# The first output projection in three split passes, its differential half begun inside the attention

## The chip, the cores and the metric

The kernel runs on one core of a Trainium2 chip, in one launch. The metric is the device time of that core in microseconds (us), the median of the runs. Five engines run their own instruction streams and meet at semaphores: TensorE (PE: matmuls and transposes, operands from SBUF, results into one of eight PSUM banks), VectorE (DVE), ScalarE (ACT), GpSimd (POOL) and SyncE (SP: it issues DMAs from memory in the order of its program, and a wait in it holds all loads behind it).

## The reference, cut to what matters

Two layers of a transformer over 256 latent tokens and 256 context tokens, model width 1024, all in float32. The even layer computes

- `qa, ka, va, qb, kb, vb = split(t @ w_in)`, with a root-mean-square norm per head of 64 on the queries and keys;
- eight neighbourhood attention heads with a position bias and a mask, and four differential heads: `pd = softmax(q0 k0) - lam * softmax(q1 k1)`, `out_b = rms_norm(pd @ vb, subln_g) * (1 - lam_init)`;
- `y = concat(out_a, out_b) @ w_out`, with `w_out` 1024 x 1024, for latent and context tokens alike (512 columns together);
- `x = x + gate * y`, a norm over the width, a modulation per token group, and a dense SwiGLU of width 2816.

The odd layer has two other attentions, its own output projection and a choice of two of eight experts. The change is about the line `y = concat(out_a, out_b) @ w_out` of the even layer.

## The kernel before, in words

Everything is held transposed: activations are `[128 partitions, 8 tiles k, 512 tokens]`, a weight tile 128 x 128 is the stationary operand and 512 tokens are the moving one. A product in full float32 is one matmul call, which TensorE runs as two passes. A product in split form takes each operand as a high part, which is the value rounded into the type fp32r, and a low part, which is the remainder; three matmuls (high times high, low times high, high times low) go into the same bank. The first input projection (L1825 to L1827), the feed-forward part (`split3`, L1979 to L1981) and the experts are in split form; the attentions and both output projections (`out_pe`, L1945) are in full float32. ACT makes a high part with a copy (L1094, L1125), DVE the low part with a subtraction (L1503, L1530).

Weights pass through a ring of four slots of 2 MB. `order` lists the loads and `slot_of` the slot of each; SP waits for the work named in `released` that frees a slot. Behind the six chunks of the input projection come ("O0", 0) and ("O0", 1), the halves of `w_out` by output columns, then ("F0", 0), the first gate and up chunk of the feed-forward part in slot 2, ("A0b", 6), a chunk of modulation weights in slot 3, ("F0", 1), and so on.

The attention A0 is a list of 36 jobs, written out by `att_plan`: jobs 0 to 15 are differential pairs, the rest pairs of neighbourhood heads, and in between jobs 22, 25, 28 and 31 are "sub" jobs, one for each of the four token tiles, which norm that tile's differential output and turn it. Tiles 0 and 1 attend to 512 keys, 2 and 3 to 256. The loop of each engine goes through steps i: PE computes the scores of job i (L1890), turns the probabilities (or the sub's data) of job i-3 into banks 4 and 5 (L1907), and multiplies job i-4 with the values (L1925, L1929) into bank 6 or 7. ACT copies what was turned in job i-3 (L1038; for a sub into `hT` k = 4 to 7, L1031), takes the exponentials of job i (L1048), and copies a finished tile of head outputs into `hT` k = 0 to 3 (L1063). DVE takes the maxima of job i (L1406), mixes the pair of job i-2 (L1414), takes the reciprocals of job i-1 (L1421) or norms the sub of job i-1 (L1430, L1431), and POOL scales the probabilities of the head jobs (L885).

Then `out_pe` waits for all outputs and makes eight output tiles d, each over the eight k, in banks 0 to 3, with w_out in full float32. `out_dve` adds each tile, times its gate, to the stream (L1453) and sums squares (L1460 to L1463). While that runs ACT makes the high parts of the first two feed-forward units (`unit_high`, 128 x 1024 each), and DVE, ahead of `out_dve`, their low parts (`unit_low`, L1530) and twelve accumulation steps of modulation weights (`modulate(0)` to `modulate(2)`, L1267, L1270). The norm follows (PE L1781, ACT L950, DVE L1559), then the modulated tokens in high and low parts (L1564, ACT L1134, L1571), for which the first feed-forward matmuls wait.

```
jb = job_at(pl, i - LAG_TURN)
if jb is not None:
    pe.wait_ge(s["copied"], jb["banks0"])
...
att_pe("A0")
out_pe("O0", "A0", S_ALL, 4)
norm_pe("n01", S_ALL, sq[0])
```

Of the kernel before, what the change touches and what calls it, by code (L numbers as in the profile page):

```python
# [37 lines left out]
P = 128  # L38
# [33 lines left out]
UF = 2  # L72
# [74 lines left out]
def build_kernel(nc, a, out):  # L147
    with ExitStack() as ctx:
# [64 lines left out]
        assert 16384 == (KT + 2 * HALF_T[0]) * S_ALL  # L213
        whi = sb("whi", [P, URING, UNIT], F32R)
# [103 lines left out]
        L0_SLOTS = [0, 1, 2, 2, 0, 2, 1, 2, 0, 2, 1, 2]  # L318
# [3 lines left out]
        for j in range(6):  # L322
            order += [("F0", j), dsum[j]]
# [69 lines left out]
        for nm in ("O0", "O1"):  # L393
            outp[nm] = {k: sem(f"out{nm}_{k}") for k in ("done", "added")}
        f_hi = sem("ffn_unit_high_ready")
# [125 lines left out]
        def piece_lo(c, i):  # L521
            return ring012r[:, slot_of(at["W0", c]), i * FU:(i + 1) * FU]

# [116 lines left out]
        def att_plan(layer):  # L640
# [39 lines left out]
            pairs = groups = banks = mixes = scales = 0  # L680
            for jb in jobs:
                jb["pair"], jb["group"], jb["banks0"] = pairs, groups, banks
# [36 lines left out]
        def _(sp):  # L719
# [15 lines left out]
            for g, (nm, j) in enumerate(order):  # L735
# [12 lines left out]
                elif nm == "F0":  # L748
                    load(g, slot3(g, 256)[:, 0:KT, :], cols(a["ffn_w_gate"], 256 * j, 256))
# [188 lines left out]
        def _(act):  # L938
# [80 lines left out]
            def att_act(nm, between=lambda i: None):  # L1019
                s, pl = att[nm], plans[nm]  # L1020
                for i in range(NSTEP[nm]):
# [5 lines left out]
                    if jb is not None:  # L1027
                        for e in range(2 if jb["kind"] == "head" else 1):
                            act.wait_ge(s["turned"], jb["banks0"] + e + 1)
                            if jb["kind"] == "sub":  # L1030
                                act.activation(hT[:, 4:8, jb["t"] * P:(jb["t"] + 1) * P],  # L1031
# [21 lines left out]
                    if jb is not None and jb["last"]:  # L1053
# [8 lines left out]
                        else:  # L1062
                            act.activation(hT[:, 4 * jb["half"]:4 * jb["half"] + 4, t * P:(t + 1) * P],  # L1063
# [52 lines left out]
            att_act("A0")  # L1116
# [116 lines left out]
        def _(dve):  # L1233
# [156 lines left out]

            def att_dve(nm):
                s, pl = att[nm], plans[nm]
                for i in range(NSTEP[nm] + 1):
# [40 lines left out]
                    if jb is not None and jb["last"] and jb["kind"] == "diff":  # L1434
# [3 lines left out]
                        dve.tensor_reduce(ssf[:, 4 * t:4 * t + 4], v3(osq, P), AX.X, ALU.add).then_inc(s["ored"], 1)  # L1438
                    if nm == "A0" and i == ROOT_STEP:
# [5 lines left out]
            def out_dve(nm, l, nc_, after):  # L1445
# [3 lines left out]
                for d in range(KT):  # L1449
# [9 lines left out]
                    if d == 0:  # L1459
                        ch.after(dve.tensor_tensor(sq[0][:, 0:nt], x, x, ALU.mult))  # L1460
                        continue
                    ch.after(dve.tensor_tensor(sq[1][:, 0:nt], x, x, ALU.mult))
                    ins = dve.tensor_tensor(sq[0][:, 0:nt], sq[0][:, 0:nt], sq[1][:, 0:nt], ALU.add)  # L1463
                    if d == KT - 1:
                        ins.then_inc(norm[after]["square"], 1)
                    else:
                        ch.after(ins)
# [85 lines left out]
            for u in range(UF):  # L1553
                unit_low(u)
# [681 lines left out]
```

## Time and profile before

| | |
|---|---|
| median of 3 runs | 1923.04 us (1920.83 to 1923.13) |
| the profiled execution's own time | 1919.05 us |
| its span, first to last instruction | 1917.2 us |
| mean granted TensorE clock | 0.984 of full |
| busy: PE, DVE, ACT, POOL | 1827.5, 1358.9, 1106.5, 176.0 us |
| attention A0, PE's first score to the first output matmul | 215.28 to 304.95 us |
| output projection O0 on PE | 304.95 to about 360.2 us |
| first feed-forward matmul | 371.4 us |
| experts, from about 941 us on | one item takes about 118.5 us, PE busy throughout |

The profile is one execution; times are counted from its first instruction. A busy time of PE sums matmuls whose ends are modelled, so intervals between starts tell its pace better than durations. Idle time stands in square brackets with what ended it.

### The profile page before, as it was taken

The numbers are of one execution on the slowest core, as the hardware profiler recorded it, in microseconds if no ns is written. First come the engines' busy times: TensorE is split into PE (matmuls) and PEld (weight loads), VectorE is DVE, ScalarE is ACT, GpSimd is POOL, SyncE is SP. The second block draws the span as 40 slices with busy tenths as digits, with TensorE's granted clock in tenths as the row PEclk, the third lists the DMA queues.
The fourth block names the chain that finished last, engine by engine and source line by source line (L and its number), as shares of the span: only waits on it lengthen the run. The fifth ranks groups of instructions, "written<-read, shape, count | busy, mean of one in ns | idle before, by whom it ended". The sixth has DMA issues, their size and how long they took to land.

```text
span 1917.2 us, 24691 instructions
## 1 busy us (share of the span) xinstructions
PE 1827.5 (95%) x8660; PEld 1434.4 (75%) x8660; DVE 1358.9 (71%) x1733; ACT 1106.5 (58%) x1488; POOL 176.0 (9%) x253
## 2 busy tenths in 40 slices
PE   5999889799999999899899999999999999999999
PEld 2777564388888887557788888888888888888877
DVE  2534575567645555352699899998989989899897
ACT  3423483132222222365488888888888877887784
POOL 0114331011100100432100000000000000000010
PEclk8999999899999999999899999999999999999999
DMA  9344500478464552130399999999999999999995
GB/s 357 107 176 165 176 1 9 145 279 291 143 202 138 186 187 85 44 133 1 134 370 373 375 390 373 384 375 384 384 377 385 373 372 384 382 387 375 384 366 204
DMA packets 231538, 496.38 MB, mean 259 GB/s; under 512 B 6065, under 2 KB 43953, under 8 KB 231473
## 3 DMA queue, kind: packets, MB, share of 16 engines
q1 hardware_dynamic: 227936, 488.53, 69.6%
q0 software_dynamic: 1920, 5.77, 0.9%
q10 hardware_dynamic: 1616, 1.22, 0.2%
q8 instruction: 40, 0.66, 0.1%
q14 instruction: 26, 0.21, 0.0%
HBM read 475.05 MB, written 20.45 MB: 258 GB/s over the span
## 4 chain that ended last, share of the span: by engine, by line
PE 84%; DVE 5%; ACT 3%; DMA 3%; issue 2%; POOL 1%; SPq 1%; DVEq 0%; ACTq 0%; POOLq 0%
PE ps L2142 9%; PE ps L2144 9%; PE ps L2143 9%; PE ps L1979 6%; PE ps L1981 6%; PE ps L1980 6%; PE ps L2156 5%; PE ps L2154 5%; PE ps L2155 5%; PE ps L1945 4%; PE ps L1871 2%; PE ps L1825 2%; DMA ring<-in_moe_w 2%; PE ps L1827 2%; PE ps L1826 2%
## 5 line engine op out<-in xcount | busy, mean ns | idle before, releaser
L1617 DVE TENSOR_TENSOR wlo<-ring,whi 128x1024 fp32r<-128x1024 f32 x672 | 795.9, 1226 | 87.6 <-ACT whi L1170 78.3
L1170 ACT ACTIVATE whi<-ring 128x1024 fp32r<-128x1024 f32 x672 | 691.6, 1057 | 182.8 <-DMA ring<-in_moe_w 81.0
L2142 PE MATMUL ps<-whi,xgr 128*128 128x512 f32 x896 | 354.1, 395 | 1.5 <-DVE xgr L1695 1.5
L2144 PE MATMUL ps<-whi,xgr 128*128 128x512 f32 x896 | 350.0, 391 | 0.0
L2143 PE MATMUL ps<-wlo,xgr 128*128 128x512 f32 x896 | 349.4, 390 | 0.0
L2144 PEld LDWEIGHTS ps<-whi,xgr 128*128 128x128 f32 x896 | 168.6, 188 | 36.0
L2142 PEld LDWEIGHTS ps<-whi,xgr 128*128 128x128 f32 x896 | 168.6, 188 | 35.1 <-issue 1.7
L2143 PEld LDWEIGHTS ps<-wlo,xgr 128*128 128x128 f32 x896 | 168.8, 188 | 33.7
L1125 ACT ACTIVATE fsa<-ring 128x1024 fp32r<-128x1024 f32 (+2 forms) x76 | 71.8, 946 | 192.6 <-PE ps L1981 192.6
L2154 PE MATMUL ps<-whi,hidr 128*128 128x512 f32 x448 | 175.9, 393 | 0.0
L2156 PE MATMUL ps<-whi,hidr 128*128 128x512 f32 x448 | 174.5, 390 | 0.0
L2155 PE MATMUL ps<-wlo,hidr 128*128 128x512 f32 x448 | 174.4, 389 | 0.0
L1979 PE MATMUL ps<-hTh,fsa 128*128 128x512 f32 x352 | 139.9, 398 | 8.5 <-DVE hTl L1571 8.5
L1981 PE MATMUL ps<-hTl,fsa 128*128 128x512 f32 x352 | 137.8, 392 | 0.0
L1270 DVE SCALAR_TENSOR_TENSOR scr<-ring,scond,scr 128x512 f32<-128x512 f32 x140 | 99.4, 746 | 1.1
L1530 DVE TENSOR_TENSOR fsa<-ring,fsa 128x1024 fp32r<-128x1024 f32 (+2 forms) x38 | 42.9, 1128 | 80.4 <-ACT fsa L1125 80.3
L1530 DVE TENSOR_TENSOR fsb<-ring,fsa 128x1024 fp32r<-128x1024 f32 (+2 forms) x38 | 41.2, 1085 | 81.8 <-ACT fsa L1125 81.8
L2156 PEld LDWEIGHTS ps<-whi,hidr 128*128 128x128 f32 x448 | 84.1, 188 | 17.6
L2155 PEld LDWEIGHTS ps<-wlo,hidr 128*128 128x128 f32 x448 | 84.2, 188 | 17.0
L2154 PEld LDWEIGHTS ps<-whi,hidr 128*128 128x128 f32 x448 | 84.1, 188 | 16.8
L1979 PEld LDWEIGHTS ps<-hTh,fsa 128*128 128x128 f32 x352 | 66.5, 189 | 26.7 <-issue 8.3
L1945 PE MATMUL ps<-hT,ring 128*128 128x512 f32 (+1 forms) x256 | 84.6, 488 | 1.4 <-ACT hT L1063 1.4
(271 smaller groups left out, 2560.1 us busy)
## 6 DMA issues: line engine op xcount, KB each, us to landing
ring<-in_moe_w SPq DMA_DIRECT2D x168, 2048.0 KB, 9.8
ring<-in_ada_w SPq DMA_DIRECT2D x24, 2048.0 KB, 12.7
ring<-in_ev_w_in SPq DMA_DIRECT2D x6, 2048.0 KB, 8.0
ring<-in_ffn_w_gate SPq DMA_DIRECT2D x11, 1024.0 KB, 5.4
ring<-in_ffn_w_up SPq DMA_DIRECT2D x11, 1024.0 KB, 8.0
expert_tokens<-work SPq DMA_DIRECT2D x2, 3072.0 KB, 17.7
ring<-in_ffn_w_down SPq DMA_DIRECT2D x4, 1536.0 KB, 8.7
ring<-in_ffn_w_down SPq DMA_DIRECT2D x4, 1280.0 KB, 8.4
```

What stands on the lines that cost most here:

```text
L1170: act.activation(whi[:, u % URING, :], mslot[(u // 4) % MRING][:, (u % 4) * UNIT:(u % 4 + 1) * UNIT], ACT.Copy).then_inc(m_hi, 1)
L1617: dve.tensor_tensor(wlo[:, u % URING, :], mslot[(u // 4) % MRING][:, (u % 4) * UNIT:(u % 4 + 1) * UNIT], whi[:, u % URING, :].bitcast(F32) ...
L1945: ins = pe.matmul(ps[d % nb][:, 0:nt], w[:, k, (d % 4) * P:(d % 4 + 1) * P], hT[:, k, 0:nt], start=(k == 0), stop=(k == KT - 1))
L1979: pe.matmul(bank, wh, xh, start=first, stop=False)
L1980: pe.matmul(bank, wl, xh, start=False, stop=False)
L1981: return pe.matmul(bank, wh, xl, start=False, stop=last)
L2142: pe.matmul(bank[:, :], xgr[:, 0, kk, :], hi[:, ws], start=(kk == 0), stop=False)
L2143: pe.matmul(bank[:, :], xgr[:, 0, kk, :], lo[:, ws], start=False, stop=False)
L2144: ins = pe.matmul(bank[:, :], xgr[:, 1, kk, :], hi[:, ws], start=False, stop=(kk == KT - 1))
L2154: pe.matmul(ps[z][:, :], hidr[:, 0, f, :], hi[:, ws], start=(f == 0), stop=False)
L2155: pe.matmul(ps[z][:, :], hidr[:, 0, f, :], lo[:, ws], start=False, stop=False)
L2156: ins = pe.matmul(ps[z][:, :], hidr[:, 1, f, :], hi[:, ws], start=False, stop=(f == FTE - 1))
```

## The change

O0 is computed in split form. Its weight half 0 is split during the attention: ACT writes the high parts (128 x 1024, four pieces) in its steps 4, 6, 8 and 10 into ring slot 2, and DVE overwrites the weights in slot 0 with the low parts in its steps 26, 28, 30 and 32. Half 1 is split after the attention, the high parts into the place of the attention's values (`o0wh`). The attention's outputs go into `hTh` (fp32r), and DVE makes their low parts `outl` out of PSUM: for each sub (`sub_lo`) and each tile of head outputs (`out_lo`). PE may not turn into bank 4 again before `sub_lo`, and not begin the group of values after next before `out_lo`.

In PE's steps 36 to 39 the differential half (k = 4 to 7) of output tiles 0 to 3 is computed, one tile a step, ahead of that step's turn and values. After the attention come the head halves (k = 0 to 3) of tiles 0 to 3, then tiles 4 to 7 whole.

Since slot 2 holds the high parts, ("F0", 0) is loaded only after four output tiles, and SP's order is now ("A0b", 6), ("F0", 0), ("F0", 1), ... The first two feed-forward units' low parts move behind output tile 5, `modulate(0)` and `modulate(1)` behind tiles 3 and 4, and `modulate(2)` behind the modulated tokens.

Added and removed lines, with 8 spaces of indentation taken off:

```diff
@@ -211,6 +211,10 @@
+with ExitStack() as scope:
+    scope.enter_context(nc.sbuf_tensor("below_values", [P, SLOT + 8192], F32))
+    o0wh = scope.enter_context(nc.sbuf_tensor("o0wh", [P, SLOT], F32R))
@@ -315,11 +319,12 @@
-L0_SLOTS = [0, 1, 2, 2, 0, 2, 1, 2, 0, 2, 1, 2]
+L0_SLOTS = [0, 1, 2, 2, 0, 2, 1, 2, 0, 2, 1, 2] + [0, 1, 3, 2]
-for j in range(6):
+order += [dsum[0], ("F0", 0)]
+for j in range(1, 6):
@@ -392,6 +397,10 @@
+o_hi = sem("output_weights_high_ready")
+o_lo = sem("output_weights_low_ready")
+sub_lo = sem("differential_outputs_low_ready")
+out_lo = sem("head_outputs_low_ready")
@@ -520,6 +529,19 @@
+def o_piece(h, i):
+    return piece(at["O0", h], i)
+def o_piece_hi(h, i):
+    return (o0wh if h else ring012r[:, slot_of(at["F0", 0]), :])[:, i * FU:(i + 1) * FU]
+def o_piece_lo(h, i):
+    return ring012r[:, slot_of(at["O0", h]), i * FU:(i + 1) * FU]
+outl = hidh[:, 0:KT, :]
@@ -677,8 +699,11 @@
-    pairs = groups = banks = mixes = scales = 0
+    pairs = groups = banks = mixes = scales = subs = 0
+        jb["subs"] = subs
+        subs += jb["kind"] == "sub"
@@ -746,6 +771,9 @@
+            if j == 0:
+                sp.wait_ge(outp["O0"]["done"], 4)
@@ -1028,7 +1056,7 @@
-                        act.activation(hT[:, 4:8, jb["t"] * P:(jb["t"] + 1) * P],
+                        act.activation(hTh[:, 4:8, jb["t"] * P:(jb["t"] + 1) * P],
@@ -1060,7 +1088,7 @@
-                    act.activation(hT[:, 4 * jb["half"]:4 * jb["half"] + 4, t * P:(t + 1) * P],
+                    act.activation((hTh if nm == "A0" else hT)[:, 4 * jb["half"]:4 * jb["half"] + 4, t * P:(t + 1) * P],
@@ -1113,7 +1141,20 @@
-    att_act("A0")
+    def output_hi(h, i):
+        if i == 0:
+            g = at["O0", h]
+            act.wait_ge(slot_full[slot_of(g)], 16 * loads_upto(g))
+        act.activation(o_piece_hi(h, i), o_piece(h, i), ACT.Copy).then_inc(o_hi, 1)
+    def between(i):
+        if i in (4, 6, 8, 10):
+            output_hi(0, (i - 4) // 2)
+    att_act("A0", between)
+    for i in range(4):
+        output_hi(1, i)
@@ -1387,6 +1428,11 @@
+    def output_low(h, i):
+        dve.wait_ge(o_hi, 4 * h + i + 1)
+        dve.tensor_tensor(o_piece_lo(h, i), o_piece(h, i), o_piece_hi(h, i).bitcast(F32), ALU.subtract)\
+           .then_inc(o_lo, 1)
@@ -1436,13 +1482,28 @@
+            if nm == "A0" and i in (26, 28, 30, 32):
+                output_low(0, (i - 26) // 2)
+            jb = job_at(pl, i - LAG_TURN)
+            if jb is not None and jb["kind"] == "sub":
+                ts = slice(jb["t"] * P, (jb["t"] + 1) * P)
+                dve.wait_ge(s["copied"], jb["banks"])
+                dve.tensor_tensor(outl[:, 4:8, ts], v3(ps[4][:, :], P), hTh[:, 4:8, ts].bitcast(F32), ALU.subtract)\
+                   .then_inc(sub_lo, 1)
+            jb = job_at(pl, i - LAG_PV - 1)
+            if nm == "A0" and jb is not None and jb["last"] and jb["kind"] == "head":
+                ts = slice(jb["t"] * P, (jb["t"] + 1) * P)
+                dve.wait_ge(s["out"], jb["t"] + 1)
+                dve.tensor_tensor(outl[:, 0:4, ts], v3(ps[6 + jb["group"] % 2][:, :], P),
+                                  hTh[:, 0:4, ts].bitcast(F32), ALU.subtract).then_inc(out_lo, 1)
-    def out_dve(nm, l, nc_, after):
+    def out_dve(nm, l, nc_, after, between=lambda d: None):
@@ -1456,15 +1517,14 @@
-            if d == 0:
-                ch.after(dve.tensor_tensor(sq[0][:, 0:nt], x, x, ALU.mult))
-                continue
-            ch.after(dve.tensor_tensor(sq[1][:, 0:nt], x, x, ALU.mult))
-            ins = dve.tensor_tensor(sq[0][:, 0:nt], sq[0][:, 0:nt], sq[1][:, 0:nt], ALU.add)
-            if d == KT - 1:
-                ins.then_inc(norm[after]["square"], 1)
-            else:
-                ch.after(ins)
+            ch.after(dve.tensor_tensor(sq[min(d, 1)][:, 0:nt], x, x, ALU.mult))
+            if d:
+                ins = dve.tensor_tensor(sq[0][:, 0:nt], sq[0][:, 0:nt], sq[1][:, 0:nt], ALU.add)
+                if d == KT - 1:
+                    ins.then_inc(norm[after]["square"], 1)
+                else:
+                    ch.after(ins)
+            between(d)
@@ -1550,11 +1610,17 @@
-    for u in range(UF):
-        unit_low(u)
-    for v in range(UF + 1):
-        modulate(v)
-    out_dve("O0", 0, 2, "n01")
+    for i in range(4):
+        output_low(1, i)
+    def between(d):
+        if d in (3, 4):
+            modulate(d - 3)
+        if d == 5:
+            for u in range(UF):
+                unit_low(u)
+    out_dve("O0", 0, 2, "n01", between)
@@ -1571,8 +1637,7 @@
+    modulate(2)
@@ -1893,6 +1958,8 @@
+                if nm == "A0" and jb["subs"]:
+                    pe.wait_ge(sub_lo, jb["subs"])
@@ -1917,6 +1984,8 @@
+                        if nm == "A0":
+                            pe.wait_ge(out_lo, g - 1 - pl["squares"])
@@ -1929,6 +1998,17 @@
+    def out0_tile(d, ks):
+        h = d // 4
+        for k in ks:
+            ws = slice(k % 2 * 512 + d % 4 * P, k % 2 * 512 + (d % 4 + 1) * P)
+            wh, wl = o_piece_hi(h, k // 2)[:, ws], o_piece_lo(h, k // 2)[:, ws]
+            pe.matmul(ps[d % 4][:, :], wh, hTh[:, k, :], start=(k == 4), stop=False)
+            pe.matmul(ps[d % 4][:, :], wl, hTh[:, k, :], start=False, stop=False)
+            ins = pe.matmul(ps[d % 4][:, :], wh, outl[:, k, :], start=False, stop=(k == 3))
+        return ins
@@ -1969,8 +2049,30 @@
-    att_pe("A0")
-    out_pe("O0", "A0", S_ALL, 4)
+    NJ = len(plans["A0"]["jobs"])
+    def between(i):
+        d = i - NJ
+        if not 0 <= d < 4:
+            return
+        if d == 0:
+            pe.wait_ge(o_lo, 4)
+            pe.wait_ge(sub_lo, 4)
+        if d in (0, 2):
+            pe.wait_ge(att["A0"]["exp"], 2 * len(plans["A0"]["pairs"]) - 2 + d)
+        out0_tile(d, range(4, KT))
+    att_pe("A0", between=between)
+    pe.wait_ge(att["A0"]["out"], plans["A0"]["outs"])
+    pe.wait_ge(out_lo, 4)
+    for d in range(KT):
+        if d == 4:
+            pe.wait_ge(o_lo, 8)
+        if d >= 4:
+            pe.wait_ge(outp["O0"]["added"], d - 3)
+            out0_tile(d, range(4, KT))
+        out0_tile(d, range(4)).then_inc(outp["O0"]["done"], 1)
```

## Rows read from the trace of the kernel before

**Rows 1.** Windows of core 0: busy us (instructions) by engine, then granted clock, DMA share, GB/s
```profile
281.00:299.00 18.00, 17.66 (x163) 11.74 (x161) 10.29 (x29) 14.78 (x49) 8.26 (x16) 1.00 0.00 1
299.00:305.00 6.00, 4.33 (x45) 2.97 (x45) 0.38 (x3) 4.18 (x15) 2.81 (x5) 1.00 0.01 3
305.00:361.00 56.00, 55.15 (x128) 24.19 (x128) 25.56 (x43) 3.07 (x3) 0.00 (x0) 1.00 0.12 38
...
1030.00:1148.00 118.00, 118.00 (x540) 97.73 (x539) 107.09 (x102) 94.36 (x103) 0.00 (x0) 1.00 1.02 376
```

**Rows 2.** The chain that ended last, by time: start, length, what
```profile
304.95 55.22 PE ps L1945 x128
360.26 0.89 DVE xT L1453 x2
```

**Rows 3.** Timeline of the first feed-forward units on PE: start, us, engine, line, what
```profile
385.18 0.39 PE L1979 MATMUL ps<-hTh,fsa 128*128 128x512 f32 x1
...
390.62 0.39 PE L1979 MATMUL ps<-hTh,fsa 128*128 128x512 f32 x1
```

**Rows 4.** Timeline of PE at the attention's end
```profile
298.28 0.66 PE L1907 MATMUL ps<-cst,scr 128*128 128x128 f32 x4
299.76 0.66 PE L1907 MATMUL ps<-cst,scr 128*128 128x128 f32 x4 [0.82 <-ACT scr L1038]
300.35 0.66 PE L1929 MATMUL ps<-scr,work 128*64 128x128 f32 x8
...
304.95 0.70 PE L1945 MATMUL ps<-hT,ring 128*128 128x512 f32 x1 [0.70 <-ACT hT L1063]
```

**Rows 5.** Lines by themselves: count, duration ns min/median/max, starts, forms
```profile
L1094 ACT ACTIVATE ring_high<-ring x12: 1041/1052/1057, 68.7 to 189.5; 128x1024 fp32r<-128x1024 f32 x12
L1063 ACT ACTIVATE hT<-ps x8: 597/608/615, 278.5 to 901.6; 128x512 f32<-128x512 f32 x8
L1503 DVE TENSOR_TENSOR ring_low<-ring,ring_high x12: 1215/1218/1226, 69.8 to 190.7; 128x1024 fp32r<-128x1024 f32 x12
```

**Rows 6.** Groups by form: count, busy us, mean ns, idle before
```profile
L1584 DVE TENSOR_TENSOR scr<-scr,ps 128x512 f32<-128x512 f32 x22 | 15.0, 680 | 0.0
```

**Rows 7.** Timeline of ACT in the attention's steps around 5 to 11
```profile
227.52 0.60 ACT L1038 ACTIVATE scr<-ps 128x512 f32<-128x512 f32 x1 [0.61 <-PE ps L1907]
...
245.96 0.38 ACT L1038 ACTIVATE scr<-ps 128x256 f32<-128x256 f32 x1 [0.39 <-PE ps L1907]
```

**Rows 8.** Timeline of DVE in steps 27 to 33
```profile
284.97 0.75 DVE L1406 TENSOR_REDUCE nmx<-ps 128x1 f32<-128x256 f32 x2
...
287.48 0.17 DVE L1421 RECIPROCAL rsum<-sums 128x2 f32<-128x2 f32 x1 [1.69 <-ACT scr L1048]
...
293.55 0.76 DVE L1406 TENSOR_REDUCE nmx<-ps 128x1 f32<-128x256 f32 x2 [0.79 <-PE ps L1890]
```

**Rows 9.** Timeline of PE: the turns of jobs 26 and 29
```profile
289.00 0.66 PE L1907 MATMUL ps<-cst,scr 128*128 128x128 f32 x4
...
293.45 0.66 PE L1907 MATMUL ps<-cst,scr 128*128 128x128 f32 x4
```

**Rows 10.** Timeline of POOL and DVE in the feed-forward part
```profile
393.88 1.29 POOL L903 TENSOR_TENSOR hidl<-scr,hidh 128x512 fp32r<-128x512 f32 x1 [89.80 <-ACT hidh L1140]
394.78 1.48 DVE L1530 TENSOR_TENSOR fsa<-ring,fsa 128x1024 fp32r<-128x1024 f32 x1 [1.65 <-ACT fsa L1125]
```

**Rows 11.** DMA issues by line from 190 to 260 us: count, KB, median us to landing
```profile
ring<-in_ffn_w_up SPq DMA_DIRECT2D x1, 1024.0 KB, 12.7
```

**Rows 12.** The page's costliest groups, columns as in rows 6
```profile
L1270 DVE SCALAR_TENSOR_TENSOR scr<-ring,scond,scr 128x512 f32<-128x512 f32 x140 | 99.4, 746 | 1.1
```

**Rows 13.** Timeline of DVE ahead of unit 2's low part
```profile
383.74 1.22 DVE L1530 TENSOR_TENSOR fsa<-ring,fsa 128x1024 fp32r<-128x1024 f32 x1 [2.15 <-ACT fsa L1125]
```

**Rows 14.** Timeline of PE behind the bias addition of step 8
```profile
239.69 0.98 PE L1907 MATMUL ps<-cst,scr 128*128 128x128 f32 x4 [3.36 <-DVE scr L1414]
```

**Rows 15.** Windows, columns as in rows 1
```profile
371.40:376.00 4.60, 4.55 (x9) 2.50 (x9) 4.60 (x13) 2.90 (x7) 0.00 (x0) 0.50 0.91 373
```

## The prediction

> **What bounds the kernel now.** I read four views. The windows came first: in the stretch of the change PE is the busiest engine, 17.66 of 18 us in the last full steps of the attention, 4.33 of 6 in its tail, and the whole of the output projection [rows 1]. In the experts PE is busy 118.00 of 118 us, and nothing there starts before the work ahead of it; so what is taken out here moves the rest forward as a block. The chain of waits came second: all 55.22 us of O0 stand on it, from 304.95 us, and DVE's add follows the last matmul at 360.26 [rows 2]. Third, the timelines of PE, DVE and ACT between 281 and 305 us, to see who has room for the added work: PE none before 299, DVE is busy 10.29 of 18 us, ACT 14.78 [rows 1]. Last, the issues of SP and the landing of DMAs.
>
> **The matmuls.** O0 is 128 passes in 55.2 us, 0.431 each, two to a product: 0.863 us [rows 2]. In split form a unit of 24 matmuls with the same 512 columns runs from 385.18 to 390.62, 0.2267 us each, so a product is 0.680 us [rows 3]. All 64: 192 x 0.2267 = 43.5 us, 11.7 less.
> The page "FP8 and Floating Point Precision" of the Trainium skill, in its section "TensorE Precision Notes", says that true FP32 takes four passes through the array. Three for four would leave 41.4 us and make the sum 2.1 us better; the measured paces of the two forms decide, and they say 43.5.
>
> **The part that goes under the attention.** 48 of the 192 matmuls, 10.9 us, are in steps 36 to 39. Before, PE ends the turn of job 32 at about 298.9 (298.28 and 0.6, the distance from a turn to the next group) and O0 starts at 304.95: 6.05 us, with seven more groups of turns and values at about 0.6 us [rows 4], 4.2 us, and idle time that waits for ACT's copies (0.82) and for the last output copy (0.70). With the change the tiles stand between these groups, so ACT's copies lie beside them: 10.9 + 4.2 = 15.1 us. After the last values come ACT's output copy, 0.61 [rows 5], and now DVE's low part out of PSUM, 0.68 [rows 6], with the hand-overs 1.45 us instead of 0.70. Then 144 matmuls, 32.65 us. From 298.9 on that is 15.1 + 1.45 + 32.65 = 49.2 us against 6.05 + 55.2 = 61.25: **12.1 us less** (12.05), if the steps up to 36 stay where they are.
> They don't.
>
> **ACT's four high parts of half 0**, 1.05 us each [rows 5], stand behind the exponentials of steps 4, 6, 8 and 10. In the steps around 5 ACT waits 0.61 us for PE in every step [rows 7] and one piece comes in two steps, so it is late by 0.4 us once and has that back. The piece of step 8 falls behind the bias addition, where ACT waits for PE anyhow; that of step 10 meets 0.39 us of room [rows 7] and then steps with little. Bounds 0 and 4.2 us (all four on the path); I take 0.3, as three of the four have their room in a row.
>
> **DVE's additions** are the term on which the sum hangs: four low parts of weights, 1.22 each [rows 5], four of subs and three of head tiles at 0.68 [rows 6], 9.7 us in some 20 us, on an engine that had 7.7 us free between 281 and 299 [rows 1], but in pieces between waits. I follow the streams in order. Step 25: ACT's sub copy ends at 282.2, DVE's sub part at 282.95, PE turns job 23 about 0.2 us late. Step 26: behind the norming of the sub comes a weight part, and the maxima of job 27, at 284.97 before [rows 8], start at 286.25; its exponentials end at 288.15 and the reciprocal, 287.48 before with 1.69 us of idle time ahead of it [rows 8], starts at 288.2. Step 28: weight part to 289.55, sub part to 290.25, and only then PE may turn job 26 into bank 4: 290.3 against 289.00 [rows 9], 1.3 late. Step 29: maxima to 290.95, norming to 292.3, head part to 292.95. Step 30: maxima, reciprocal, weight part to 295.0. Step 31: ACT, late with the exponentials of job 30 (to 294.85), copies the sub to 295.4, DVE's part ends at 296.1, PE turns job 29 at 296.15 against 293.45 [rows 9], 2.7 late. Steps 32 to 34: maxima 296.85, norming 298.2, weight part 299.4, the maxima of job 33 to 300.15, its exponentials to 301.3, ACT's sub copy 301.9, DVE's part 302.6; PE turns job 32 at 302.65 against 298.28 [rows 4]. **4.4 us late** at the place where the first tile starts. Behind the tiles, which take 2.7 us each, DVE catches up. Bounds: 0, if the free time took everything, and 9.7, all of it in series.
> In one place of the trace a DVE subtraction of this form runs beside a POOL instruction, and takes 1.48 us where it otherwise takes 1.22 [rows 5, 10]. POOL scales head probabilities just behind each reciprocal, where the weight parts stand; two such meetings are 0.5 us.
> The page "GPSIMD Engine Reference" of the Trainium skill ("8. Key points") says that POOL shares its SBUF interfaces with VectorE and that they contend when a DVE instruction has two SBUF inputs. A weight part has two, a sub or head part one. The trace agrees with 1.48 against 1.22.
> So the stretch to step 36 grows by 0.3 + 4.4 + 0.5 = 5.2 us.
>
> **Half 1 of the weights.** ACT starts after its last output copy, four at 1.05; DVE's four low parts end about 6 us after the attention. PE needs them at tile 4, 10.9 us after its start: cost 0, with 4.9 us of room, and at most what DVE needs beyond that. DVE then adds tiles at 2.4 us each (two at 0.48, two at 0.69) where PE needs 2.7 and then 5.4.
>
> **What moves past queues.** ("F0", 0) goes to SP only at the fourth tile, 21.8 us before O0's end, with ("F0", 1) behind it, and then as before the modulation chunk and the zero fills. Before, with others in flight, its second DMA landed 12.7 us after issue [rows 11]. ACT's two high parts and DVE's last low part take 3.4 us, and DVE adds tile 6 (2.4 us) before it can take the last tile: 21.8 - 3.4 - 2.4 = 16.0 us for the landing. Cost 0 at 12.7, one for one beyond 16; bounds 0 and 2.5, the latter for a landing half as long again. `modulate(0)` and (1), eight steps of 0.746 [rows 12], lie between tiles for which PE needs 5.4 us. `modulate(2)`, four of them, 3.0 us, comes before unit 2's low part, where DVE stood idle for 2.15 us and which ended at 384.96 [rows 13]: 0.85 late, to 385.8. PE is on unit 1 until 387.9 (the first of [rows 3] is its thirteenth matmul, twelve at 0.2267 from its end). Cost 0; 0.85 at most. ("A0b", 6) loads a little earlier than before: 0. The norm after the last tile has the same instructions.
>
> **The sum.** -12.1 + 5.2 = -6.9 us. The profiled execution, 1919.05 us with a span of 1917.2, would come to 1912.1; it is 4.0 under the median of 1923.04, so the prediction for the median is 1923.0 - 6.9 = **1916.1 us**. A measurement of this kernel can tell about 0.2%, 3.85 us, from no change.
>
> **The rivals.**
> *DVE's work finds its room.* The waits before maxima and reciprocals [rows 8] take it up, and step 36 is at most 0.6 us late: -11.5, 1911.5 us. For it: 7.7 us free. Against: the idle pieces lie before instructions that then hold up ACT. Chance 0.18.
> *DVE becomes the bound of the late steps.* All 9.7 us in series, and 0.8 for the others: -12.1 + 10.5 = -1.6, 1921.4 us, no difference. For it: each sub forms a ring DVE, PE, ACT, DVE. Against: the four waits I followed each absorb something. Chance 0.13.
> *The clock falls in the attention.* The same rings, but each makes PE stand as at step 8, where 3.36 us of idle time was followed by a group of 0.98 us that is 0.66 otherwise [rows 4, 14]: TensorE was at its lower level, 1.2 GHz. A late step has three groups at 0.6 us, 1.8, and as much again at half rate. Four such steps, 7.2, and a first tile in a stretch like 371.4 to 376, 4.6 us at a granted clock of 0.50 [rows 15], half of which is lost, 2.3: 9.5 on top of the case before: +7.9, 1930.9 us, slower. It decides once a sub's wait makes PE stand as long as at step 8; I found at most 1.3 us, and 0.82 at job 33 left the clock at 1.00 [rows 1, 4]. Chance 0.05.
> *The first feed-forward chunk is late.* Landing 18.5 us after issue instead of 12.7: 2.5 us back, -4.4, 1918.6 us. Chance 0.05.
> *The split saves nothing*, because the weight loads of three matmuls, mixed with the turns, don't hide: 11.7 back, +4.8, 1927.8 us. The pace of 0.2267 includes a weight load for each matmul [rows 3]. Chance 0.03.
>
> **How the numbers follow.** The forecast has 0.56, with its own range from -9 to -4.5. Faster: 0.56 + 0.18 + 0.05, less 0.02 for the scatter of 2.3 us among the runs before, 0.77; same 0.13 + 0.02, 0.15; slower 0.05 + 0.03, 0.08. The range goes from 1910.5, which takes in the case in which DVE's work costs nothing, to 1921.0, which takes in half of the case in which DVE is the bound; some 0.15 is left out.
>
> **What would show it.** 24 matmuls of O0 in 5.44 us; the first output tile starting about 5.2 us later than 298.9; PE idle before the turns of jobs 26, 29 and 32 for DVE's sub parts; from the last values to the head halves 1.45 us; O0's end near 353.3 instead of 360.2, and the first feed-forward matmul near 364.5. If the turn of job 32 stays at 298.3, the first rival holds; if it is at 307 or the clock shows under 1.00 there, the second or the third. If O0 ends at 353 but the feed-forward part starts later than 12 us after, it is the load. If the experts begin 6.9 us earlier and the end doesn't, the block did not move as one, and I am wrong about the part behind.

## The result and the profile after

| | before | after |
|---|---|---|
| median | 1921.93 us (1918.89 to 1923.81, 6 runs) | 1911.15 us (1909.31 to 1915.59, 6 runs) |
| profiled execution, its span | 1919.05, 1917.2 us | 1909.31, 1907.5 us |
| mean granted TensorE clock | 0.984 | 0.982 |

The ratio is 0.995, 95% interval 0.9934 to 0.9965: faster by 0.5%, 10.8 us between the medians and 9.7 us between the spans, where 6.9 were forecast.

To follow the 9.7 us I cut both spans at places that exist in both. The first cut is the turn of job 22, the first sub: up to there nothing of the change stands on PE, only ACT's high parts. All figures are differences of start times, in us.

| stretch | before | after | difference | forecast |
|---|---|---|---|---|
| first instruction to the first score | 215.28 | 215.76 | +0.48 | 0 |
| first score to the turn of job 22 | 65.35 | 65.35 | 0.00 | +0.3 |
| turn of job 22 to the turn of job 32 | 17.65 | 20.24 | +2.59 | +4.9 |
| turn of job 32 to the last tile's add | 61.98 | 50.48 | -11.50 | -12.05 |
| last add to the first feed-forward matmul | 11.18 | 10.27 | -0.91 | 0 |
| from there to the end | 1545.76 | 1545.40 | -0.36 | 0 |
| sum | 1917.2 | 1907.5 | -9.7 | -6.9 |

The page's first section of the changed kernel: a longer busy time on every engine but PE, which has 8.9 us less (before: 1827.5).

```profile
PE 1818.6 (95%) x8724; PEld 1448.7 (76%) x8724; DVE 1373.6 (72%) x1749; ACT 1114.1 (58%) x1496; POOL 177.7 (9%) x253
```

Windows of the changed kernel, columns as in [rows 1]: the late steps, and O0 behind the attention.

```profile
281.50:299.50 18.00, 16.40 (x155) 11.00 (x153) 16.66 (x34) 12.48 (x42) 8.24 (x13) 1.00 0.00 1
...
318.80:351.80 33.00, 32.89 (x144) 26.95 (x144) 26.98 (x41) 6.24 (x7) 0.00 (x0) 1.00 0.40 128
```

DVE, busy 10.29 of 18 us before [rows 1], is now busy 16.66 and PE has gone from 17.66 to 16.40: for these 18 us DVE is the bound. In the last window PE works without a gap, 144 matmuls in 33.0 us.

PE's timeline, columns as in [rows 4]. In this order: the turns of jobs 22, 26, 29 and 32 (before: 280.63, 289.00, 293.45, 298.28), the first matmul of the tiles, the first of the head halves, the matmuls of the norm, and the first one of the feed-forward part.

```profile
281.11 0.66 PE L1974 MATMUL ps<-cst,work 128*128 128x128 f32 x4
...
290.20 0.63 PE L1974 MATMUL ps<-cst,scr 128*128 128x128 f32 x4 [0.53 <-issue]
...
295.39 0.63 PE L1974 MATMUL ps<-cst,scr 128*128 128x128 f32 x4 [0.69 <-POOL scr L913]
...
301.35 0.63 PE L1974 MATMUL ps<-cst,scr 128*128 128x128 f32 x4 [0.56 <-issue]
301.74 0.47 PE L2008 MATMUL ps<-hTh,ring_low 128*128 128x512 f32 x1
...
318.83 0.47 PE L2008 MATMUL ps<-hTh,ring_low 128*128 128x512 f32 x1 [1.51 <-DVE hidh L1498]
...
354.22 1.12 PE L1846 MATMUL ps<-scr,ones 128*128 128x512 f32 x2 [2.49 <-DVE scr L1522]
362.10 0.76 PE L2081 MATMUL ps<-hTh,fsa 128*128 128x512 f32 x1 [6.76 <-DVE hTl L1637]
```

The chain of waits of the changed kernel (start, length, what) shows who owns which stretch: DVE from 288 to 299 with hardly a step of another engine between, then PE, one hand-over through ACT and DVE at 317.4, and PE again to the last add.

```profile
288.25 1.25 DVE ring_low L1434
289.50 0.60 DVE hidh L1492
...
317.37 0.61 ACT hTh L1091
318.00 0.70 DVE hidh L1498
...
351.83 0.89 DVE xT L1514 x2
```

### The profile page after: what moved, and what is told of

It is laid out like the page before. It is cut to its first block, busy times and chain, and to the rows that moved or that the text cites. A ratio compares the mean times of both kernels' runs of the same rounds, so it can differ in the third digit from the quotient of the medians.

```text
span 1907.5 us, 24845 instructions
## 1 busy us (share of the span) xinstructions
PE 1818.6 (95%) x8724; PEld 1448.7 (76%) x8724; DVE 1373.6 (72%) x1749; ACT 1114.1 (58%) x1496; POOL 177.7 (9%) x253
## 3 DMA queue, kind: packets, MB, share of 16 engines
q10 hardware_dynamic: 1616, 1.22, 0.2%
## 4 chain that ended last, share of the span: by engine, by line
PE 87%; DVE 5%; ACT 3%; DMA 2%; issue 1%; POOL 1%; SPq 1%; DVEq 0%; ACTq 0%; POOLq 0%
PE ps L2244 10%; PE ps L2246 10%; PE ps L2245 10%; PE ps L2081 6%; PE ps L2083 6%; PE ps L2082 6%; PE ps L2258 5%; PE ps L2257 5%; PE ps L2256 5%; PE ps L1936 2%; PE ps L1890 2%; PE ps L1892 2%; PE ps L1891 2%; PE ps L1955 2%; PE ps L2025 1%
```

## The experiments

There were eleven runs; e10 is the changed kernel again and e12 is e6 again. All are read by the same cuts; whole times of single executions are told too, but they don't decide, for a reason given at the end of this section. "1 to 22" is from the first score to the turn of job 22, and so on; where an expectation counts from the first score to the last add, it is the column of that name, and up to the turn of job 32 it is the sum of the first two.

| kernel | 1 to 22 | 22 to 32 | 32 to last add | first score to last add | last add to feed-forward |
|---|---|---|---|---|---|
| before | 65.35 | 17.65 | 61.98 | 144.98 | 11.18 |
| after | 65.35 | 20.24 | 50.48 | 136.07 | 10.27 |
| e1 no overlap | 65.28 | 20.24 | 51.08 | 136.60 | 10.26 |
| e2 low parts elsewhere | 65.29 | 19.08 | 50.41 | 134.78 | 10.74 |
| e3 low parts doubled | 65.33 | 25.64 | 50.47 | 141.44 | 11.05 |
| e4 tile 3 last | 65.28 | 20.24 | 48.71 | 134.23 | 10.49 |
| e5 reductions instead | 65.28 | 20.38 | 50.50 | 136.16 | 10.27 |
| e6 = e2 and e4 | 65.28 | 19.09 | 48.73 | 133.10 | 10.26 |
| e7 two products of three | 65.29 | 20.23 | 41.33 | 126.85 | 11.21 |
| e8 subs in bank 5 | 65.28 | 19.61 | 50.98 | 135.87 | 10.26 |
| e10 after, again | 66.23 | 20.27 | 50.48 | 136.98 | 11.21 |
| e11 = e2, e4 and e8 | 63.93 | 18.42 | 48.85 | 131.20 | 10.26 |
| e12 = e6, again | 65.33 | 19.10 | 48.72 | 133.15 | 10.27 |

**e1: the split form without the part under the attention.**

```diff
-att_pe("A0", between=between)
+att_pe("A0")
+pe.wait_ge(o_lo, 4)
+pe.wait_ge(sub_lo, 4)
...
-    if d >= 4: out0_tile(d, range(4, KT))
+    out0_tile(d, range(4, KT))
     out0_tile(d, range(4)).then_inc(outp["O0"]["done"], 1)
```

> All 192 matmuls of O0 stand behind the attention; the rest is as in the changed kernel. Measured from the attention's first score to the first add behind O0's last tile: 144.98 us before, 136.07 changed. Theory A, the early half only fills idle time of the tail: before, PE had 6.05 us there with 4.2 us of its own work, so 10.9 us of matmuls fit into 1.85 us of idle time and push the rest. Without them from the turn of job 32 to the start of O0 6.67 + 0.8 us, then 192 x 0.2267 = 43.5: some 51.1 us against 50.5 changed, so 136.7, the span 0.6 to 1.1 us longer. Theory B, the overlap is what brings the gain: some 9 us come back, 145.

Measured: 51.08 from the turn of job 32, 0.60 more than with the overlap (1910.64 us, beside 1920.5 for the kernel before). Placing 10.9 us of matmuls under the attention brings 0.6 us, because PE had next to nothing free there. What the work fills are two waits for ACT's copies, 0.54 and 0.21 us in e1. The largest piece of idle time, 1.51 us ahead of the head halves, stands in e1 and in the changed kernel alike (318.83 above); e4 is about it.

```profile
302.89 0.66 PE L1974 MATMUL ps<-cst,scr 128*128 128x128 f32 x4 [0.54 <-ACT scr L1066]
...
304.35 0.66 PE L1974 MATMUL ps<-cst,scr 128*128 128x128 f32 x4 [0.21 <-ACT scr L1066]
...
308.89 0.47 PE L2008 MATMUL ps<-hTh,ring_low 128*128 128x512 f32 x1 [1.51 <-DVE hidh L1498]
```

The gain is the pace: before to e1 the stretch is 10.9 us shorter. O0 itself, from its first matmul to the last add, takes 43.9 us instead of 55.3, 11.4 less, and 0.5 is lost ahead of it, where DVE's part is now in the open (a wait of 1.51 instead of 0.70 us) and ACT's copies hold PE 0.3 us less.

**e2: two low parts of weights at step 21, two at steps 37 and 38.** There is an early place: at step 21 DVE waits for ACT's root of the differential outputs, and all high parts have been there since step 10.

```diff
-if nm == "A0" and i in (26, 28, 30, 32):
-    output_low(0, (i - 26) // 2)
...
 if nm == "A0" and i == ROOT_STEP:
...
+    output_low(0, 2)
+    output_low(0, 3)
+if nm == "A0" and i in (37, 38):
+    output_low(0, i - 37)
...
```

> The weights' low parts leave DVE's steps 26 to 32: those of k = 4 to 7 come in step 21, where DVE stood idle 3.55 us behind ACT's table loads, those of k = 0 to 3 in steps 37 and 38. From the first score to the turn of job 32: 83.00 us before, 85.59 changed. Theory A, DVE's weight parts make most of the lateness: 83.8 to 84.3, the span 1.3 to 1.8 us shorter than changed. Theory B, the waits for the subs' low parts make it, whatever else DVE does: 85.4 to 85.6, nothing gained.

Measured: 19.08 against 20.24, so the four parts cost 1.16 us where they stood (their meetings with POOL, which go with them, included), and none in their new places (1 to 22 unchanged, 32 to the last add 50.41). The late steps in e2, DVE at 12.98 instead of 16.66 us:

```profile
283.70:301.70 18.00, 16.60 (x154) 10.95 (x150) 12.98 (x34) 13.63 (x46) 7.77 (x16) 1.00 0.01 1
```

The whole time was 1916.04 us, above the changed kernel's, with a longer stretch of experts (919.5 us instead of 914.8); see the end of the section.

**e3: each of these four subtractions done twice.**

```diff
 if nm == "A0" and i in (26, 28, 30, 32):
+    dve.wait_ge(o_hi, 4)
+    ch.after(dve.tensor_tensor(etab[:, 0:FU], o_piece(0, (i - 26) // 2), o_piece_hi(0, (i - 26) // 2).bitcast(F32), ALU.subtract))
     output_low(0, (i - 26) // 2)
```

> Each of the four weight parts in DVE's steps 26 to 32 is computed twice (the first time into an unused place). Theory A, DVE is the bound of the late steps: 4 x 1.2 us more, of which the first may find room: first score to turn of job 32 at 89.2 to 90.4 instead of 85.59, span 3.5 to 4.8 longer, and PE's idle time ahead of the turns of jobs 26, 29 and 32 grows by it. Theory B, the waits between take it up: under 86.6. If the clock falls in these stands, more than 91.

Measured: 25.64, 5.40 more than after, for 4.88 us of added instructions (four at 1.22). The first set of four cost 1.16, the second all of itself and 0.5 more. The free time was used up by the first. The excess comes with a fall of the clock: the stand in front of one turn reached 3.21 us, and the groups behind it take 1.09 to 1.22 us where they take 0.63 to 0.70 at the full clock; from 291.8 to 294.3 us the granted clock was 0.50. That all of the 0.5 is the clock is argued, not shown.

```profile
292.11 1.09 PE L1976 MATMUL ps<-cst,scr 128*128 128x128 f32 x4 [3.21 <-issue]
293.12 1.22 PE L1957 MATMUL ps<-work 64*128 64x256 f32 x4
...
298.07 0.70 PE L1957 MATMUL ps<-work 64*128 64x256 f32 x4
```

That is the mechanism of the rival with the falling clock; it occurred only with DVE's added weight work doubled.

**e4: the fourth half tile behind the last values**, so that PE works while ACT copies the last outputs and DVE takes their low part.

```diff
-    if not 0 <= d < 4:
+    if not 0 <= d < 3:
...
 att_pe("A0", between=between)
+out0_tile(3, range(4, KT))
```

> Output tile 3's differential half goes behind the last values instead of ahead of them, so that ACT's copy and DVE's low part of the last head tile (1.5 us, in which PE stands) lie beside its 2.7 us of matmuls. Theory A: the stand goes, span 1.4 us shorter than changed. Theory B: PE waits for something else at that place (the last probabilities' copy ahead of the last values, or the bank): the same time as changed, within 0.3.

Measured: 48.71 against 50.48, 1.77 less: the wait of 1.51 us is gone, and the other 0.26 were not taken apart. PE's rows there follow without a wait:

```profile
313.58 1.26 PE L1998 MATMUL ps<-scr,work 128*64 128x128 f32 x16
314.77 0.50 PE L2008 MATMUL ps<-hTh,ring_low 128*128 128x512 f32 x1
```

**e5: e2, and in the old steps a reduction of the same length with one SBUF input**, to ask whether it is DVE's time or its meeting with POOL that delays.

```diff
+if nm == "A0" and i in (26, 28, 30, 32):
+    dve.tensor_reduce(rsum_x[:, (i - 26) // 2:(i - 26) // 2 + 1], o_piece(0, 0), AX.X, ALU.max)
```

> As e2_low_early, and in DVE's steps 26, 28, 30 and 32, where the weight parts stood, a maximum over 1024 elements of one SBUF operand (about 1.2 us, nothing uses it). It separates DVE's time from the meeting with POOL: in the changed kernel POOL took 2.80 and 2.73 us for four scalings (1.84 before, 1.84 in e2) beside weight parts, which have two SBUF operands. First score to turn of job 32: 85.59 changed, 84.37 in e2. Theory A, it is DVE's time: 85.2 to 85.6, with POOL's four at 1.84 again. Theory B, it is the meeting: 84.4 to 84.7.

Measured: 20.38, close to the 20.24 with the subtractions, and POOL's four scalings are back at 1.84 us. The row is e5's, for the set that took 2.80 us in the changed kernel.

```profile
289.47 1.84 POOL L914 TENSOR_SCALAR scr<-scr,rsum 128x256 f32<-128x256 f32 x4 [3.25 <-DVE rsum L1468]
```

The place is not quite the old one: the reductions stand behind the sub and head parts of their step, the subtractions stood ahead of them. In step 28 DVE therefore waits 0.43 us for ACT's copy with the reduction still to come, and its next maxima start 3.84 us behind those of job 27, where it is 3.44 in the changed kernel. Behind that, one row of the changed kernel is longer than its counterpart in e5 (second fence), a multiplication of two SBUF inputs that runs beside POOL's set of 2.73 us:

```profile
295.87 0.92 DVE L1476 TENSOR_TENSOR work<-work,rs 128x512 f32<-128x512 f32 x1
```

```profile
298.24 0.68 DVE L1477 TENSOR_TENSOR work<-work,rs 128x512 f32<-128x512 f32 x1
```

So 0.40 is lost by the place and 0.24 won by the missing meeting, which makes the 0.14 between the two. DVE's time makes most of the delay, and the meetings some 0.24 us of it.

**e6 and e12: e2 and e4 together**, once and then in five rounds.

> e2_low_early and e4_tile3_last together. The two gains are at different places (1.29 us in steps 26 to 36, 1.84 behind the last values), so they add: from the first score to the last add 136.07 - 1.29 - 1.84 = 132.9. The rival: the weight parts that e2 put into steps 37 and 38 now meet the last head tile's low part and hold it up, 133.4 to 134.2.

> e6_both, timed: 133.1 us from first score to last add again, 3 us under the changed kernel; ratio to the kernel before about 0.9937.

Measured: 133.10 and 133.15, from job 22 on 67.82 both times: 2.9 less than the change, where e2 and e4 alone have 1.23 and 1.77 (69.49 and 68.95 against 70.72). The two are additive. The whole time is told below.

**e7: high weights times low tokens left out**, so O0 has 128 matmuls instead of 192 and its result is of less precision. It asks how far PE's pace still sets the end.

```diff
-    pe.matmul(ps[d % 4][:, :], wl, hTh[:, k, :], start=False, stop=False)
-    ins = pe.matmul(ps[d % 4][:, :], wh, outl[:, k, :], start=False, stop=(k == 3))
+    ins = pe.matmul(ps[d % 4][:, :], wl, hTh[:, k, :], start=False, stop=(k == 3))
```

> O0 without its third product (high weights times low tokens): 64 matmuls less, 16 of them in the attention's tail. Theory A, O0 is bound by PE alone: 64 x 0.2267 = 14.5 us less, 121.6 from the first score to the last add. Theory B, DVE or the first feed-forward chunk is close behind: DVE needs some 31.5 us from the last head tile on (four weight parts 4.6, eight tiles of 2.3 with two of 2.7 and one of 2.4 more), which gives 131; and the chunk lands 8.3 us after the fourth tile and then needs 5.8 more where only 14.5 are left.

Measured: the last add at 126.85, between the two numbers. PE ends as the first theory has it, but the norm's matmuls stand 7.9 us behind it, where it was 2.49 in the changed kernel: DVE's adds, low parts and modulation steps run back to back from 317 us on, and the norm waits for them. PE's rows, then DVE's, in e7:

```profile
338.40 0.39 PE L2009 MATMUL ps<-hTh,ring_low 128*128 128x512 f32 x1
346.67 2.07 PE L1846 MATMUL ps<-scr,ones 128*128 128x512 f32 x2 [7.88 <-DVE scr L1522]
```

```profile
340.80 1.22 DVE L1590 TENSOR_TENSOR fsb<-ring,fsa 128x1024 fp32r<-128x1024 f32 x1
...
343.56 0.69 DVE L1522 TENSOR_TENSOR scr<-scr 128x512 f32<-128x512 f32 x1
344.29 0.88 DVE L1514 SCALAR_TENSOR_TENSOR xT<-ps,ada,xT 128x256 f32<-128x256 f32 x2
```

So the changed O0 has 136.07 - 126.85 = 9.2 us until DVE's own work is the bound.

**e8: the subs are turned into bank 5**, so that only the second head of the next job waits for DVE's low part.

```diff
-ins = pe.transpose(ps[4 + e][:, c * P:(c + 1) * P], data[:, c * P:(c + 1) * P], ident)
+bk = 5 if jb["kind"] == "sub" else 4 + e
+ins = pe.transpose(ps[bk][:, c * P:(c + 1) * P], data[:, c * P:(c + 1) * P], ident)
...
```

ACT's copy and DVE's part read bank 5 as well, and PE's wait for `sub_lo` stands before the second half of a turn.

> The changed kernel with the subs turned into bank 5 instead of 4, so that only the second half of the next turn waits for DVE's low part of a sub. 85.59 us from the first score to the turn of job 32 in the changed kernel. Theory A, DVE's own stream is the bound there (it stands in the chain from 288.2 to 299.0 without a pause): at most 0.4 less. Theory B, the wait of the turns for the subs' low parts is: 1 us or more less.

Measured: 19.61, 0.63 less by this cut. But the cut flatters e8: the turn of job 32 begins with the half that need not wait and has the wait inside it, so that it takes 1.02 us instead of 0.63. The first matmul of the tiles is the better mark. It starts 20.46 us behind the turn of job 22 (301.36 less 280.90), in the changed kernel 20.63 (301.74 less 281.11): 0.17 us less, and 0.13 at the last add (70.59 against 70.72). By the mark of the expectation (84.89 from the first score) it would lie between the two theories; by the first tile the first one holds: beside the weight parts DVE's own stream is the bound. PE's rows of e8, the two halves of job 26's turn, where PE stands 0.24 instead of 0.53 us, then job 32's turn and the first tile:

```profile
289.27 0.44 PE L1975 MATMUL ps<-cst,scr 128*128 128x128 f32 x2
289.94 0.44 PE L1975 MATMUL ps<-cst,scr 128*128 128x128 f32 x2 [0.24 <-DVE hidh L1492]
...
300.51 1.02 PE L1975 MATMUL ps<-cst,scr 128*128 128x128 f32 x4
301.36 0.48 PE L2009 MATMUL ps<-hTh,ring_low 128*128 128x512 f32 x1
```

**e11: all three, and e10: the changed kernel again**, in the same rounds as e12.

> e2_low_early, e4_tile3_last and e8_bank5 together. Measured alone they took 1.29, 1.84 and 0.20 us off the 136.07 from first score to last add, the first two together 2.97. Theory A, DVE is no longer the bound once the weight parts are gone, and the wait for the subs' low parts is what is left of the lateness (84.37 against 83.00): the third now brings 0.5 to 1.2, 131.9 to 132.6. Theory B, it brings 0.2 again: 132.9. Against the kernel before 12 to 13 us less: ratio about 0.9935; against the changed kernel 3 to 4 us less.

> The changed kernel once more, beside the next two, to compare whole times. Every theory: 136.1 us from the first score to the last add, as in its first profile; against the kernel before 8.9 us less up to there and 0.9 more where the norm's matmuls find the full clock, so a ratio of 0.9950 to 0.9955; a stage may differ by 0.1, the experts by 2 or 3 us from run to run.

Measured: 131.20 and 136.98, each outside what I had expected, e11 by 0.7 below and e10 by 0.9 above. The column "1 to 22" says why: it is 65.3 in eleven profiles, 63.93 in e11 and 66.23 in e10, before any edit has an effect. With 65.3 in front, e11 would have 132.6. Every one of the thirteen has PE stand for 3.36 us behind the bias addition of step 8 [rows 14]; what the clock does there differs. First e11, then e10:

```profile
239.67 0.63 PE L1977 MATMUL ps<-cst,scr 128*128 128x128 f32 x4 [3.36 <-DVE scr L1460]
240.13 1.06 PE L1997 MATMUL ps<-work,scr 128*128 128x128 f32 x8
241.12 0.70 PE L1957 MATMUL ps<-work 64*128 64x256 f32 x4
```

```profile
240.97 1.08 PE L1974 MATMUL ps<-cst,scr 128*128 128x128 f32 x4 [3.36 <-DVE scr L1460]
...
243.69 1.23 PE L1955 MATMUL ps<-work 64*128 64x256 f32 x4
```

In e11 the granted clock stays at 1.00 through the stand and behind it. In e10 it is 0.50 already during the last microsecond of the stand and up to 5.2 us behind its end. In the other eleven it falls to 0.50 within 0.7 us behind the end and is back at 1.00 by 4.1 us behind it. The first group alone doesn't tell them apart: it takes 0.63 us in e1 too, and the one behind it 1.84 where e11 has 1.06.

```profile
240.60 0.63 PE L1974 MATMUL ps<-cst,scr 128*128 128x128 f32 x4 [3.36 <-DVE scr L1460]
241.06 1.84 PE L1994 MATMUL ps<-work,scr 128*128 128x128 f32 x8
```

Counted from job 22, e11 is at the first matmul of the tiles after 18.96 us, e12 after 19.48: 0.52 for bank 5, and 0.55 at the last add (67.27 against 67.82). So bank 5 is worth three times as much once the weight parts are gone.

**The whole times.** In five rounds on one chip:

| kernel | median (lowest to highest) | ratio to before, 95% |
|---|---|---|
| e10, the change | 1914.5 us (1911.9 to 1916.19) | 0.9957 (0.9944 to 0.997) |
| e11, all three | 1908.95 us (1906.22 to 1910.42) | 0.9926 (0.9913 to 0.9938) |
| e12, e2 and e4 | 1907.44 us (1905.8 to 1909.13) | 0.9922 (0.991 to 0.9935) |

Both new versions beat the change and the kernel before (1921.63 us there), with intervals apart from e10's. Which of the two is better isn't told by this. The change itself is 7.1 us under the kernel before in these rounds, where it was 10.8 in the first ones: so much do medians of five or six runs move. The profiled executions of e10 and e12 are 9.4 us apart (1914.1 and 1904.7), though the edits are worth 2.9 (70.75 less 67.82 from job 22 on). The clock behind step 8 and at the norm accounts for 0.9 each, and the experts for 3.9: their stretch, from the first to the last start of their first matmul line, was 918.8 us in e10 and 914.9 in e12, and no edit touches them; 0.8 are spread over the rest. It was so with e2: waits of ACT from 945 to 1862 us, in total, times, longest; the changed kernel's and then e2's.

```profile
ACT whi L1211 <- DMA ring<-in_moe_w: 74.1, 66, 5.7
```

```profile
ACT whi L1211 <- DMA ring<-in_moe_w: 127.6, 103, 5.7
```

## Why the prediction was right, step by step

**The number.** The median came out 5 us under the 1916.1 of the forecast and 0.65 us above the lower end of the range, beside the 1911.5 of the first rival, whose mechanism did not occur. That is in part luck: in the later rounds the same kernel was 7.1 us under the one before, which is near the 6.9 of the forecast. The cuts decide: 8.9 us up to the last add where 6.9 were forecast.

**The matmuls and the part under the attention: right.** 12.05 forecast, 11.50 measured. From the turn of job 32 to the head halves it took 318.83 - 301.35 = 17.48 us where 0.6 + 15.1 + 1.45 = 17.15 were forecast, and the head part 33.0 where 32.65 were. My working didn't say how much of it is the overlap's; e1 gives the overlap 0.6 and the split form 10.9.

**ACT's high parts: 0, not 0.3.** First score to the turn of job 22 is 65.35 in both kernels; all four found room.

**DVE's additions: the mis-sized term.** Forecast 4.4 and 0.5 for meetings with POOL; measured 2.59 for both. The mechanism held: DVE's parts delay the turns behind the subs, each a little more. The turns of jobs 26, 29 and 32 are 0.72, 1.46 and 2.59 us later than before, counted from job 22, where I had 1.3, 2.7 and 4.4. The step that was wrong is in the working of steps 26 and 27, the maxima that "start at 286.25" and the exponentials that "end at 288.15": I let ACT begin when both maxima were done, 1.90 us from the start of the maxima to the end of the exponentials. ACT begins after the first. DVE's and ACT's rows of the changed kernel, step 27:

```profile
285.45 1.22 DVE L1434 TENSOR_TENSOR ring_low<-ring,ring_low 128x1024 fp32r<-128x1024 f32 x1
286.59 0.75 DVE L1452 TENSOR_REDUCE nmx<-ps 128x1 f32<-128x256 f32 x2
...
288.17 1.33 DVE L1434 TENSOR_TENSOR ring_low<-ring,ring_low 128x1024 fp32r<-128x1024 f32 x1
```

```profile
287.04 0.47 ACT L1076 ACTIVATE scr<-ps,nmx 128x256 f32<-128x256 f32 x1
```

The exponential starts at 287.04, while the two reductions run until 287.34. The working has this step three times, for the maxima of jobs 27, 30 and 33. In the trace they start at 286.59, 292.61 and 298.57 and the exponentials end at 288.06, 294.08 and 300.04: 1.47 us each time. That is 0.43 us in each of three rounds, 1.3 of the 1.8 between 4.4 and 2.6. The other 0.5 is likely that I added durations, where DVE's rows follow each other a little faster (0.60 us from a sub part to the maxima behind it, for a duration of 0.68); no run tests this.

Three runs take part of the 2.59 apart: 1.16 for the weight parts (e2, the meeting with POOL included); 0.52 for the wait for bank 4 once the weight parts are gone (e11 against e12, at the first tile; beside them it is 0.17, e8); and 0.9, which stays in e11 and which no run took apart. Sub and head parts still stand on DVE there, and PE waits for ACT's copy of a sub (0.19) and for DVE's part (0.29).

**Meetings with POOL: real, mostly on the other engine, and smaller than priced.** One weight part took 1.33 instead of 1.22 us and one multiplication of a norming 0.92 instead of 0.68, but POOL's scalings beside them went from 1.84 us for four to 2.80 and 2.73.

```profile
287.50 2.80 POOL L913 TENSOR_SCALAR scr<-scr,rsum 128x256 f32<-128x256 f32 x4 [3.26 <-DVE rsum L1467]
...
293.51 2.73 POOL L913 TENSOR_SCALAR scr<-scr,rsum 128x256 f32<-128x256 f32 x4 [3.21 <-DVE rsum L1467]
```

PE's turn of job 29 is put down to POOL, with 0.69 us, but DVE's part for the same bank had ended only 0.1 us earlier (294.60 and 0.69). What lay on the path is some 0.24 us, by e5, where 0.5 were forecast. The Trainium skill ("GPSIMD Engine Reference", "8. Key points") names two SBUF inputs of the DVE instruction as one of two conditions; the subtraction has two and e5's reduction one, and the rows agree with it.

**The loads: right, with more room than I gave.** The first feed-forward chunk was issued at 330.41 and ACT took it up 8.3 us later, where 16.0 were to be had. DVE still waited 3.18 us for PE before the last add. Rows of SP, ACT and DVE:

```profile
330.41 1.62 SPq L748 DMA_DIRECT2D ring<-in_ffn_w_up  x1
```

```profile
338.67 2.01 ACT L1166 ACTIVATE fsa<-ring 128x1024 fp32r<-128x1024 f32 x2 [16.92 <-DMA ring<-in_ffn_w_up]
```

```profile
351.83 0.88 DVE L1514 SCALAR_TENSOR_TENSOR xT<-ps,ada,xT 128x256 f32<-128x256 f32 x2 [3.18 <-PE ps L2010]
```

Half 1's low parts and the moved modulation cost nothing: no gap in the window of 33.0 us, and from the first feed-forward matmul to the first expert it is 580.7 us after and 581.1 before.

**The norm: 0.9 us that I did not foresee.** PE's two matmuls of the norm came behind the same stand of 2.49 us and took 1.12 us in the changed kernel (above), 2.05 in the one before:

```profile
362.64 2.05 PE L1781 MATMUL ps<-scr,ones 128*128 128x512 f32 x2 [2.49 <-DVE scr L1463]
```

The changed kernel's second profile, e10, has 11.21 in this stretch, as before. So either level occurs with the same instructions, and e4, e2 and e3 lie between them (10.49, 10.74, 11.05), and I count the change at 8.9 us up to the last add (-11.50 and +2.59) without it. Whether the higher level is likelier behind the split form is open: seven of the twelve profiles of changed versions have 10.26 or 10.27, but of the kernel before there is one.

**The rivals.** "DVE's work finds its room" (-11.5) and "DVE is the bound, all in series" (-1.6) would have the turn of job 32 at most 0.6, or 9.7 us late; 2.59 is nearer to the first, and neither held. The split saves what the pace said (e1), and the first chunk was in time. The clock stayed at 1.00 in the late steps; PE's longest stand there was 0.69 us, and in e3 the clock fell behind one of 3.21. The experts moved as a block, 914.8 against 914.9 us.

## What to carry to other kernels

Work laid under a stage in which the same engine is already full brings only the idle time that it can fill, here 0.6 us for 10.9 us of matmuls; the gain was in the cheaper form of the product. When adding instructions to a helper engine inside a pipelined loop, look first for a step in which it waits for somebody else anyway: four subtractions cost 1.16 us in the late steps and nothing at step 21 and behind step 36, and the second set in the late steps cost more than its own length. To compare versions that differ by 1 to 3 us, cut the traces at a landmark just ahead of the edit: from job 22 to the last add two executions of the same kernel agreed within 0.03 us (70.72 and 70.75; 67.82 twice), while whole times of one kernel spread by 3 to 7 us. And the landmark must mean the same in both kernels: e8 splits the very group that was the cut, and seemed to gain 0.63 us where 0.17 were real.

## What the hardware showed that I had not expected

- The same pause leaves TensorE at different levels. Around a stand of 3.36 us the granted clock stayed at 1.00 once in thirteen profiles (e11), was at 0.50 before the stand ended once (e10), and fell within 0.7 us behind its end eleven times; the landmark behind it was at 63.93, 66.23 and 65.3 us. Behind 2.49 us of standing, the norm's pair took between 1.12 and 2.08 us. Some 1 to 2 us of a difference between two profiles can be this alone.
- DVE subtractions with two SBUF inputs slowed POOL far more than themselves: 1.22 to 1.33 us on DVE, 1.84 to 2.80 on POOL. In e2 a single scaling beside two such parts was recorded with 2.43 us, where an undisturbed pair takes 0.94:

```profile
302.59 0.94 POOL L913 TENSOR_SCALAR scr<-scr,rsum 128x256 f32<-128x256 f32 x2 [0.89 <-DVE rsum L1467]
304.18 2.43 POOL L913 TENSOR_SCALAR scr<-scr,rsum 128x256 f32<-128x256 f32 x1 [0.66 <-DVE rsum L1467]
```

- The stretch of experts, the same code in all versions, lasted from 913.6 to 921.6 us. ACT's waits for weights ranged from 74.1 to 127.6 us in all, but they don't order the executions by themselves (92.7 us of waits in the longest, e11); what decides the length stays open.
